# Experts' tokens and results by indirect transfers through memory instead of 0/1 products

## The reference

```python
def moe_swiglu(h, router, w_gate, w_up, w_down):
    ...
    probs = jax.nn.softmax((ht @ router).astype(jnp.float32), axis=-1)
    vals, idx = lax.top_k(probs, TOP_K)
    wts = vals / jnp.sum(vals, axis=-1, keepdims=True)
    gates = jnp.einsum('tk,tke->te', wts, jax.nn.one_hot(idx, N_EXPERTS, dtype=jnp.float32)).astype(h.dtype)
    out = jnp.zeros_like(ht)
    for e in range(N_EXPERTS):
        out = out + gates[:, e:e + 1] * swiglu(ht, w_gate[e], w_up[e], w_down[e])
```

## Time and profile before

| | |
|---|---|
| median of 3 runs | 1426.93 us (1426.47 to 1429.4) |
| profiled execution, its own time | 1424.97 us |
| its span, first to last instruction | 1423.2 us |
| TensorE busy | 1355.0 us (95%) |
| VectorE busy | 968.0 us (68%) |
| ScalarE busy | 834.9 us (59%) |
| moved by DMA | 326.52 MB, 229 GB/s over the span |
| granted TensorE clock, mean | 0.986 |

### The profile page before, as it was taken

One profiled execution on the slowest core, in us unless ns is written; L12 is line 12 of the kernel. 1 busy time (PEld: TensorE's weight loads), 2 busy tenths in 40 slices (PEclk: granted clock), 3 DMA queues, 4 the chain that ended last, 5 costly groups with the idle time before them and its releaser, 6 DMA issues.

```text
span 1423.2 us, 17145 instructions
## 1 busy us (share of the span) xinstructions
PE 1355.0 (95%) x6424; PEld 1116.4 (78%) x6424; DVE 968.0 (68%) x983; ACT 834.9 (59%) x898; POOL 18.7 (1%) x36
## 2 busy tenths in 40 slices
PE   6999999998779999999999999999989998899998
PEld 5888888887657888888887878787867776788887
DVE  4585555456767888888979797888855665554542
ACT  6445444356646676767677777766667455644431
POOL 3000000000000000000000000000010000000000
PEclk9999999999989999999999999999999998999999
DMA  9646555542226899998989899989765233265540
GB/s 301 229 157 202 177 183 176 169 156 90 89 104 231 304 357 320 348 351 313 350 318 352 324 346 328 332 326 349 287 222 199 90 119 118 88 208 178 190 165 30
DMA packets 140932, 326.52 MB, mean 229 GB/s; under 512 B 5755, under 2 KB 13648, under 8 KB 140880
## 3 DMA queue, kind: packets, MB, share of 16 engines
q1 hardware_dynamic: 139424, 323.00, 65.0%
q0 software_dynamic: 1440, 2.81, 0.6%
q10 hardware_dynamic: 16, 0.00, 0.0%
HBM read 324.74 MB, written 1.05 MB: 229 GB/s over the span
## 4 chain that ended last, share of the span: by engine, by line
PE 86%; DVE 5%; ACT 4%; issue 2%; DMA 2%; SPq 0%; ACTq 0%; DVEq 0%
PE bank L1471 26%; PE bank L1473 25%; PE bank L1472 25%; PE bank L1808 2%; PE bank L1783 2%; DVE w_lo L310 2%; ACT w_hi L305 2%; DMA raw<-in_moe_w_down 1%; PE bank L1804 1%; PE bank L1571 1%; DMA x<-in_x 0%; PE bank L1554 0%; PE bank L2014 0%; DVE x L922 0%; PE bank L1729 0%
## 5 line engine op out<-in xcount | busy, mean ns | idle before, releaser
L310 DVE TENSOR_TENSOR w_lo<-raw,w_hi 128x2048 fp32r<-128x2048 f32 (+2 forms) x308 | 693.6, 2268 | 272.9 <-ACT w_hi L305 272.3
L305 ACT ACTIVATE w_hi<-raw 128x2048 fp32r<-128x2048 f32 (+2 forms) x308 | 582.9, 1900 | 289.8 <-PE bank L1473 275.6
L1471 PE MATMUL bank<-w_hi,xT_hi 128*128 128x512 f32 (+2 forms) x672 | 256.7, 382 | 13.2 <-issue 5.6
L1473 PE MATMUL bank<-w_hi,xT_lo 128*128 128x512 f32 (+2 forms) x672 | 254.0, 378 | 0.0
L1472 PE MATMUL bank<-w_lo,xT_hi 128*128 128x512 f32 (+2 forms) x672 | 253.7, 378 | 0.0
L1471 PE MATMUL bank<-w_hi,gT_hi 128*128 128x512 f32 x512 | 209.3, 409 | 0.0
L1473 PE MATMUL bank<-w_hi,gT_lo 128*128 128x512 f32 x512 | 200.1, 391 | 0.0
L1472 PE MATMUL bank<-w_lo,gT_hi 128*128 128x512 f32 x512 | 199.5, 390 | 0.0
L1471 PEld LDWEIGHTS bank<-w_hi,xT_hi 128*128 128x128 f32 x672 | 127.1, 189 | 37.8 <-issue 7.7
L1473 PEld LDWEIGHTS bank<-w_hi,xT_lo 128*128 128x128 f32 x672 | 127.0, 189 | 22.9
L1472 PEld LDWEIGHTS bank<-w_lo,xT_hi 128*128 128x128 f32 x672 | 127.2, 189 | 22.1
(11 more groups left out here) (358 smaller groups left out, 1354.2 us busy)
## 6 DMA issues: line engine op xcount, KB each, us to landing
raw<-in_moe_w_gate SPq DMA_DIRECT2D x64, 1024.0 KB, 5.4
raw<-in_moe_w_up SPq DMA_DIRECT2D x64, 1024.0 KB, 5.6
raw<-in_moe_w_down SPq DMA_DIRECT2D x64, 1024.0 KB, 5.5
raw<-in_w_gate_up SPq DMA_DIRECT2D x22, 1024.0 KB, 5.2
raw<-in_conv_w_in SPq DMA_DIRECT2D x12, 1024.0 KB, 8.3
raw<-in_ffn_w_gate SPq DMA_DIRECT2D x11, 1024.0 KB, 5.2
raw<-in_ffn_w_up SPq DMA_DIRECT2D x11, 1024.0 KB, 5.1
raw<-in_ffn_w_down SPq DMA_DIRECT2D x11, 1024.0 KB, 4.9
```

The source lines that it names most:

```text
L305: nc.scalar.activation(w_hi[:, slot, :n], raw[:, slot, :n], ACT.Copy).then_inc(stream.high, 1)
L310: nc.vector.tensor_tensor(w_lo[:, slot, :n], raw[:, slot, :n], w_hi[:, slot, :n].bitcast(F32), ALU.subtract).then_inc(stream.low, 1)
L1471: mm(dst, a_hi, b_hi, start=start, stop=False)
L1473: return mm(dst, a_lo, b_hi, start=False, stop=stop)
```

## The change

- Gate and up come in two groups of 1024 columns with chunks of 2 x 128 rows by 1024 columns (4 KB in a row instead of 2 KB); silu and product then come in two halves together, `e_silu` and `e_act` have two buffers. In each expert the activation turns follow gate/up chunks 9 and 10 and down chunks 0 and 1.
- VectorE works out for each token and choice a row number (`rows_of_choices`). GpSimd writes the normed tokens `h` by four indirect transfers into a scratch array in memory, whose places for experts 1 to 7 were filled with zeros before by seven transfers. In each expert SyncE loads the 128 rows of the next into `rows_in`, and TensorE turns them (`turn_rows`, two jobs). Expert 0 still has its tokens gathered by products.
- The results of experts 0 to 6 are stored by SyncE in a second scratch array. During the last expert GpSimd fetches them back for each token and choice by four indirect transfers, and VectorE adds them, times the gate, into `x` (`take_back`, four operations of 128x1024). The last expert's results still go through `put`, with the gate applied on adding; its down chunks come by halves of the columns, so that the left half is scattered ahead of the last chunk.
- `gates`, the pick turn, the scatters and the gather of the middle experts are gone. The first and the last expert stand outside the loop.

```diff
-EG = FE // HALF
-EXPERT_CHUNKS = 4 * EG + FE // 256
+EGROUPS = FE // D
+GU_CHUNKS = 2 * EGROUPS * KD // 2
+EXPERT_CHUNKS = GU_CHUNKS + FE // (2 * P)
+SLOT_ROWS = E * P
...
+def by_half(j):
+
+    return j // 2 % 2, 2 * (j // 4) + j % 2
+
...
+    if c < GU_CHUNKS:
+        g, part, q = c // KD, c // (KD // 2) % 2, c % (KD // 2)
         w = A["moe_w_up" if part else "moe_w_gate"][0]
-        v = w[bass.ds(e, 1), half * 4 * P:(half + 1) * 4 * P, g * HALF:(g + 1) * HALF]
+        v = w[bass.ds(e, 1), 2 * q * P:2 * (q + 1) * P, g * D:(g + 1) * D]
+        return v.rearrange("e (k p) n -> p (e k) n", p=P), 2, D
...
+    if down_by_half:
+        half, q = by_half(j)
+        v = w[bass.ds(e, 1), 4 * q * P:4 * (q + 1) * P, half * HALF:(half + 1) * HALF]
...
+    slots_in = nc.dram_tensor("moe_slots_in", (SLOT_ROWS + 2 * S, D), F32, kind="Internal").ap()
+    slots_out = nc.dram_tensor("moe_slots_out", (E, P, D), F32, kind="Internal").ap()
...
+                def store_rows(e):
+                    sp.wait_ge(sem("moe_y"), 1 + e)
+                    sp.dma_start(slots_out[bass.ds(e, 1), :, :].rearrange("e p d -> p (e d)"), M["y"][:, :])\
+                        .then_inc(sem("moe_rows_stored"), 16)
+
+                def load_rows(e):
+                    sp.wait_ge(sem("moe_dispatched"), 16 * 2 * T)
+                    sp.wait_ge(sem("moe_job"), GATHER_JOBS + TURNED_JOBS * (e - 1))
+                    rows = slots_in[:SLOT_ROWS, :].rearrange("(e p) d -> e p d", p=P)
+                    sp.dma_start(M["rows_in"][:, :], rows[bass.ds(e, 1), :, :].rearrange("e p d -> p (e d)"))\
+                        .then_inc(sem("moe_rows_loaded"), 16)
+
+                with sp.Fori(0, E - 1) as e:
                     for c in range(EXPERT_CHUNKS):
-                        load(MOE0 + c, e, W1, *expert_chunk(A, e, c))
+                        load(MOE0 + c, e, W1, *expert_chunk(A, e, c, False))
+                        if c == 10:
+                            store_rows(e)
+                        if c == 18:
+                            load_rows(e + 1)
+                for c in range(EXPERT_CHUNKS):
+                    load(MOE0 + c, E - 1, W1, *expert_chunk(A, E - 1, c, True))
+                    if c == 10:
+                        store_rows(E - 1)
...
+                pool.wait_ge(W1.high, start_of["ffn1_up"] + 4)
+                for e in range(1, E):
+                    small(slots_in[e * P:(e + 1) * P, :], A["shape_blank"], "blank")
                 pool.wait_ge(sem("x_updated"), before("mla", "x_updated") + 4)
                 small(M["moe_g"][:, :], A["norm_ffn"][1:2, :].partition_broadcast(P), "moe_g")
+                pool.wait_ge(sem("moe_rows_known"), 1)
+                pool.wait_ge(sem("moe_h"), T)
+                pool.wait_ge(sem("loaded_blank"), 16 * (E - 1))
+                for choice in range(2):
+                    for t in range(T):
+                        pool.indirect_dma_start(
+                            slots_in[:, :], bass.IndirectOffsetOnAxis(ap=M["row_to"][:, choice, t:t + 1], axis=0),
+                            M["h"][:, t, :], None).then_inc(sem("moe_dispatched"), 16)
+                pool.wait_ge(sem("moe_rows_stored"), 16 * E)
+                for choice in range(2):
+                    for t in range(T):
+                        pool.indirect_dma_start(
+                            returned(choice)[:, t * D:(t + 1) * D], None, slots_out.rearrange("e p d -> (e p) d"),
+                            bass.IndirectOffsetOnAxis(ap=M["row_from"][:, choice, t:t + 1], axis=0))\
+                            .then_inc(sem("moe_returned"), 16)
...
+                def silu(e, group, first=False):
+                    act.wait_ge(W1.used, MOE0 + KD * group + KD // 2 + EXPERT_CHUNKS * e)
+                    if not first:
+                        act.wait_ge(sem("moe_act_done"), 2 * group + 4 * e)
+                    for half in range(2):
+                        A_(M["e_silu"][:, half, :], bank[half][:, :], ACT.Silu).then_inc(sem("moe_silu_done"), 1)
...
                     act.wait_ge(W1.used, MOE0 + EXPERT_CHUNKS + EXPERT_CHUNKS * e)
+                    act.wait_ge(sem("moe_rows_stored"), 16 + 16 * e)
...
+                def rows_of_choices():
+                    per_expert = iota[:, :E].unsqueeze(1).broadcast_to([P, T, E])
+                    place_ = place.rearrange("p (t e) -> p t e", t=T)
+                    row, to, here, from_ = (M["row_f"][:, j, :, :] for j in range(4))
+                    aside = const[:, C_ASIDE:C_ASIDE + 2 * T].rearrange("p (c t) -> p c t", c=2)
+                    V.tensor_scalar(L[13], place_, float(P) - 0.5, float(4 * SLOT_ROWS), ALU.is_gt, ALU.mult)
+                    link(V.scalar_tensor_tensor(L[14], per_expert, float(P), place_, ALU.mult, ALU.add))
+                    link(V.tensor_tensor(L[15], L[13], L[14], ALU.add))
+                    for choice, hot in ((0, L[5]), (1, L[9])):
+                        ins = V.tensor_tensor(L[16 + choice], hot, L[15], ALU.mult)
+                    link(ins)
+                    for choice in range(2):
+                        ins = V.tensor_reduce(row[:, choice, :], L[16 + choice], AX.X, ALU.max)
+                    link(ins)
+                    V.tensor_tensor(to, row, aside, ALU.min)
+                    link(V.tensor_scalar(here, row, float(SLOT_ROWS - P) - 0.5, None, ALU.is_lt))
+                    V.tensor_copy(M["row_to"][:, :, :], to)
+                    link(V.scalar_tensor_tensor(from_, row, float(P), here, ALU.add, ALU.mult))
+                    V.tensor_copy(M["row_from"][:, :, :], from_).then_inc(sem("moe_rows_known"), 1)
...
+                def expert_act(e, group, turned):
+                    dve.wait_ge(W1.used, MOE0 + KD * (group + 1) + EXPERT_CHUNKS * e)
+                    if turned is not None:
+                        dve.wait_ge(sem("moe_job"), turned)
+                    for half in range(2):
+                        dve.wait_ge(sem("moe_silu_done"), 2 * group + half + 1 + 4 * e)
+                        V.tensor_tensor(M["e_act"][:, half, :], bank[2 + half][:, :], M["e_silu"][:, half, :],
+                                        ALU.mult).then_inc(sem("moe_act_done"), 1)
+
...
+                def take_back(choice, t):
+                    dve.wait_ge(sem("moe_returned"), 16 * 2 * T)
+                    V.scalar_tensor_tensor(x[:, t, :], returned(choice)[:, t * D:(t + 1) * D], M["mix"][:, choice, t:t + 1],
+                                           x[:, t, :], ALU.mult, ALU.add).then_inc(sem("moe_taken_back"), 1)
+
+                def put_add(e, n, half, signal, last=False):
+                    if not (last and half == 0):
+                        dve.wait_ge(sem("moe_added"), 4 * n + 2 * half)
+                    for t in range(T):
+                        dve.wait_ge(sem("moe_put"), 4 * n + 2 * half + t + 1)
+                        xs = x[:, t, half * HALF:(half + 1) * HALF]
+                        V.scalar_tensor_tensor(xs, bank[2 * half + t][:, :], gate_of[:, t, bass.ds(e, 1)], xs,
+                                               ALU.mult, ALU.add).then_inc(sem(signal), 1)
...
+                        if last:
+                            if c == 1:
+                                pick(E - 1)
+                            if c == 4:
+                                put_copy(number, 0)
+                            if c in (11, 12, 13, 14):
+                                take_back((c - 11) // 2, (c - 11) % 2)
+                                dve.wait_ge(sem("moe_taken_back"), c - 10)
+                    put_add(e, n, 0, "moe_added", last)
...
+                def gate_up(e, c):
+                    g, up, q = c // KD, c // (KD // 2) % 2, c % (KD // 2)
+                    wide(W1, MOE0 + c, e, gth, gtl, 2 * q, (2 * up, 2 * up + 1), q == 0, q == KD // 2 - 1, tokens=1)
+
+                def expert(e, first):
+                    number = first_job(e, TURNED_JOBS)
+                    for c in range(GU_CHUNKS):
                         if c == 0:
-                            pe.wait_ge(sem("moe_drained"), PROLOGUE_JOBS - 2 + JOBS * e)
-                        if half == 0:
-
-                            pe.wait_ge(sem("moe_act_done"), max(gr, 1) + EG * e)
-                        tall(W1, MOE0 + c, e, gth, gtl, 4 * half, 4, HALF, (2 * (gr % 2) + up,), half == 0, half == 1,
-                             tokens=1)
-                        if c == 3:
+                            pe.wait_ge(sem("moe_drained"), number)
+                        if c == 0 and not first:
+                            pe.wait_ge(sem("moe_silu_done"), 4 * e)
+                        if c == 4 and not first:
+                            pe.wait_ge(sem("moe_act_done"), 4 * e)
+                        if c == 8:
+                            pe.wait_ge(sem("moe_silu_done"), 2 + 4 * e)
+                        if c == 12:
+                            pe.wait_ge(sem("moe_act_done"), 2 + 4 * e)
```

(50 more changed lines are left out.)

344 lines of the change are left out of this document (184 added, 160 removed).

## The result

| | median us | lowest to highest | ratio to before, 95% interval |
|---|---|---|---|
| before | 1426.96 | | |
| after | 1406.72 | 1401.13 to 1411.37 | 0.9853 [0.9805, 0.9901] |
| forecast | 1373.5 | range 1366 to 1402 | |

The change saves 20 us where 53.5 were forecast, and the time lies above the range. The profiled execution took 1401.13 us (span 1399.0), the shortest of the four and 23.8 less than that of before.

What follows compares the result with a forecast made beforehand. TensorE was taken to set the pace, VectorE (85%) and DMA engines (93%) close behind. Terms -48.4 - 0.4 - 1.35 - 3.3 = -53.5 came off the median 1426.93: 1373.5 us, range 1366 to 1402.

Steps and rivals of the forecast that it cites:

- TensorE's jobs in an expert, -6.92: Experts 0 to 6: scatters, gather, gates and pick turn go (7.90), two turns come (0.98); new expert 68.15 us.
- The count of weight products stays.: Experts: a wide chunk is 12 products as a tall one is, so 288 weight products stay 65.3 us.
- DMA, "no stall": Expert loads: 26.2 MB in 68.15 us needs 385 GB/s; at 388 the engines take 67.5 us, so no stall.
- Rival A: Expert stage: DMA engines become the bound, 1413 us at 357 GB/s, 1386 at 375; chance 0.20, half under 1402.
- Reserve of 0.5 us ahead of the third activation turn: VectorE's queue in experts 0 to 6: least reserve there 0.5 us, so no stall, taken as 0.
- The seven experts together: Experts 0 to 6: -6.92 us each, seven times, -48.4 us (bounds -44 to -50).
- The last expert: Jobs -5.85 us, stall ahead of the third activation turn 3.5, return transfers competing with weights 1.0: net -1.35.
- The results back in time: Last expert: GpSimd issues at 18.5 us, VectorE asks at about 36; reserve 17 us, so cost 0.
- Rivals B and D: B, results return late: 1387 us, chance 0.09. D, indirect transfers cost GpSimd too much, slower than before: chance 0.04.
- The end: After the last product: left scatter pair moves into the last expert, the gap stays: -3.3 us (-1.3 at the loop's pace).
- SyncE's queue: Experts: storing results behind load 10 and loading rows at load 18 wait for nothing; cost 0.
- the part before the experts: Products start when `gT_lo` is written, at 434.37 and not 434.83, -0.4 us; transfers of h and blanks cost 0.

Runs made afterwards that it cites:

- e7: e5 with only half of each expert weight chunk loaded (result not the reference's): 1370.89 us.
- e13: e6 with VectorE's second-group activation product ahead of chunk 18's low part and the four take_back adds behind later low parts: 1373.25 us.
- e3: The changed kernel, tensor addresses unmoved, with only half of each expert weight chunk loaded (result not the reference's): 1387.50 us.
- e12: The kernel before with only gate and up fetched as 4 KB pieces instead of 2 KB (result not the reference's): 1427.73 us.
- e5: The changed kernel with its stage regions 32 bytes lower, at the addresses of the kernel before: 1405.93 us.
- e6: e5 with gate and up fetched in 2 KB rows instead of 4 KB, products in the fitting order: 1384.30 us.
- e9: e6 with the down projection also cut from whole 4 KB rows to 2 KB rows: 1392.51 us.
- e1: The kernel before with only its stage regions moved up by 32 bytes: 1441.57 us, ratio 1.0104.
- e14: e5 with gate and up chunks fetched as whole rows of 8 KB (result not the reference's): 1387.56 us.

## Why the prediction was wrong, point by point

- **TensorE's jobs in an expert, -6.92.** Right: 68.18 us (e7), and 68.19 with the full loads (e13).
- **"The count of weight products stays."** It does, and the forecast took from it that their time stays. This step failed. A product took 0.0067 us more because four columns in `const` moved its stationary tile by 32 bytes against the weights: 1.6 us per expert (e3 against e7), some 11 in seven, about 2 in the last. Of the 8 us outside it explains some 5: about 770 products there have such a tile. The rest lies in stretches where products start 0.40 to 0.46 us apart, the granted clock at 0.50 in most of them: 32 products outside the experts in the profile of after, 11 in that of before, some 4 us more. These stretches vary from run to run: with the fast products the norm of the expert part starts anywhere from 411.50 (before) over 412.12 (e13) to 414.71 (e12, the code of before up to there), so the +3.7 alone would not show the address. No part of the prediction asked where the tensors lie. Put right alone, though, it gives nothing (e5), since the next step had failed too.
- **DMA, "no stall".** Failed too, though its figure for the capacity was right: 386 GB/s over a whole expert (e13, and 385 in e6) where the forecast put 388 as the rate of full queues with rows of 2 KB, and 385 as the need. The wrong step is the next one, that 4 KB rows "land no faster today", with no loss put down for them. The row it rests on is `w_down`, whose rows are whole; gate and up became 4 KB pieces of 8 KB rows. e12 shows them over 1 us slower. Rival A named this place, and its sign in the profile, ScalarE's waits in tens of us, is there (106 us); but e13 has the sign too (125 us) and the forecast's time, so it tells nothing by itself. Its reason, a sustained rate of 357 to 375 GB/s, is refuted. The 358 GB/s between memory and SBUF of the Trainium skill ("DMA: Bandwidth & Descriptors", section "Where 436 GB/s comes from") did not bind here either: with one core at work the windows of e6 and e13 measure 385 and 386, and that section itself has a measured 425 GB/s beside its figure.
- **Reserve of 0.5 us ahead of the third activation turn.** The place was right, and I called it "no stall". It holds only while no load is late; any late down chunk goes through `split_low` into `e_act`. In the profile that is 0.3 to 1.8 us in each of seven experts, 7 us in all: 70.82 against e3's 69.79.
- **The seven experts together:** +11.2 slow products, +7.2 waits, and -1.0 mainly because the seven of before averaged 75.26 with their loop turns, not 75.07. That is the 17.4 between -31.0 and -48.4.
- **The last expert.** Forecast stall 3.5 + 1.0; measured 9.9: 3.7 in three waits for `w_lo` between the four adds, 4.7 ahead of the third turn, and 1.5 in the 12 products behind it, at a granted clock of 0.50. The hole itself was mis-sized by 1.2; the collision, one term of 1.0, was really the 3.7; the price of the clock behind a hole was in no term. With the loads out of the way the hole is 3.3 us (e7; 2.9 in e3), so the forecast's own part, 3.4, was nearly right.
- **The results back in time.** Right: VectorE never waited for them. GpSimd issued the four at 956.85, 958.13, 960.73 and 961.97, for 0.94 to 2.29 us each; the first add stood at 976.11. But this was partly luck. The store that GpSimd waits for landed in 8.8 us (median) and not 3.9, so the issue came at 23.0 us into the expert and not at 18.5, and a transfer back took up to 12.2 us. The last result may have landed as late as 974.2, a reserve of 2 us in place of 17, and that with VectorE 6 us later than forecast. The estimate by the Trainium skill ("DMA: Bandwidth & Descriptors", section "Anatomy of one DMA") was 3.2 us to land; the trace has medians of 8.7 and 10.8 with the queues full, so it does not hold there. Rivals B and D named waits that did not come.
- **The end.** Forecast -3.3, measured 3.57 us from the last product's start to the norm's turns against 10.13: -6.6. The hole ahead of the scatters shrank from 3.52 to 1.75 us, start to start, and the two left take 1.82 us at a granted clock of 1.00; the 1.65 each of before, which the forecast carried over, stood at 0.50. This term was mis-sized in the other direction. The bound of -1.3 beside it is a slip: two scatters at the loop's pace behind the same hole take 3.52 + 1.31 of today's 10.13, which is -5.3.
- **SyncE's queue, the part before the experts.** Right: no wait for the dispatch, and -0.45 for -0.4.
- **The interval.** It reached to 1402 for rival A; two causes that add, one not seen at all, went past it.

That e13 comes out at 1373.25 against 1373.5 is partly luck: it has an order on VectorE that the forecast did not assume, and still shows experts of 69.38 and 70.34 us among those of 68.2.

What stays open: why 32 bytes matter to a product, why the 4 KB pieces are slow, why e9 is slower than e6, and how much of e5's 35 us over e7 is the lower clock behind its holes.

## What to carry to other kernels

When a change adds or widens any tensor, compare the start addresses of all operands of the inner products before and after; a product's time is part of the forecast, not a constant of the kernel. A transfer form that seems free in a kernel with slack has been measured at nothing: compare landing times of the same form, cut and stride included, at equal demand, and take a longer landing as a warning; its price has to be measured once the slack is spent (here over 1 us in a landing went with 18 to 22 us of the kernel). Price a wait of TensorE together with the clock of the products behind it. And with an in-order queue, put the work whose inputs are ready ahead of the work that waits for a load.

## What the runs showed of the hardware

- A 128x512 product takes 0.2267 us start to start when the stationary tile and the moving tile start at a distance of a multiple of 256 bytes in their partitions, and 0.2333 us at 32 or 64 bytes more (0.2323 to 0.2333 at 128): 14.6 us in a kernel of 1427 (e1). Why, and whether it is these two tiles alone, is not shown.
- Loads of 1 MiB as 4 KB pieces of 8 KB rows land in 6.5 to 6.9 us (e12) where 2 KB pieces take 5.4 to 5.6 (before); whole rows of 8 KB cost the kernel no more than 2 KB pieces (e14 against e6, 1387.56 and 1384.30 us).
- The DMA engines held 385 to 386 GB/s over experts of 68.2 us (e6, e13).
- Behind a hole of 4.92 us in TensorE's work the granted clock was 0.50, and eight products started about 0.43 us apart (after); behind holes of 3.52 us it was 0.50 (before) and of 3.55 us 1.00 (e7).
- Indirect transfers of 512 KB back from memory landed in up to 12.2 us from issue beside full load queues (after); issuing one took GpSimd 0.94 to 2.29 us.
